# First four levels of the triangular inverse on packed 32x32 diagonal blocks, with block transposes by VectorE

## What is computed

```python
    decay = jnp.exp(jnp.where(tril, gc[..., :, None] - gc[..., None, :], -jnp.inf))
    kb = kc * bc[..., None]
    a_mat = jnp.where(strict, jnp.einsum("bhncd,bhnsd->bhncs", kb, kc) * decay, 0.0)
    eye = jnp.eye(c, dtype=jnp.float32)
    t_inv = lax.linalg.triangular_solve(eye + a_mat, jnp.broadcast_to(eye, a_mat.shape), left_side=True, lower=True)
    u = jnp.einsum("bhncs,bhnse->bhnce", t_inv, vc * bc[..., None])
    w = jnp.einsum("bhncs,bhnsd->bhncd", t_inv, kb * jnp.exp(gc)[..., None])
```

## Time and profile before

| | us |
|---|---|
| median of 3 runs (lowest, highest) | 1440.19 (1439.32, 1441.13) |
| the profiled execution's own time | 1440.25 |
| its span in the profile | 1438.5 |
| PE busy | 1350.0 (94%) |
| PEld busy | 777.8 (54%) |
| VectorE busy | 463.6 (32%) |
| ScalarE busy | 295.1 (21%) |
| GpSimd busy | 24.2 (2%) |

### The profile page before, as it was taken

One profiled execution on the slowest core, in us unless ns is written; L12 is line 12 of the kernel. 1 busy time (PEld: TensorE's weight loads), 2 busy tenths in 40 slices (PEclk: granted clock), 3 DMA queues, 4 the chain that ended last, 5 costly groups with the idle time before them and its releaser, 6 DMA issues.

```text
span 1438.5 us, 19892 instructions
## 1 busy us (share of the span) xinstructions
PE 1350.0 (94%) x7689; PEld 777.8 (54%) x7689; DVE 463.6 (32%) x1023; ACT 295.1 (21%) x629; POOL 24.2 (2%) x56
## 2 busy tenths in 40 slices
PE   8999898999999999999989899898988979999997
PEld 7887777788886444444424434254342534534355
DVE  3666877764233411211202202022020211202134
ACT  4645453444212100000001000010000100101024
POOL 3000000000000000000000000000000000000000
PEclk9999999999999999999999999999999999999998
DMA  7424243563687999999999999999999999999951
GB/s 216 137 89 127 85 136 103 165 212 99 231 288 270 402 415 421 420 420 421 421 420 420 422 421 421 421 421 422 420 421 422 421 421 415 421 422 421 420 200 31
DMA packets 123126, 463.13 MB, mean 322 GB/s; under 512 B 11142, under 2 KB 70047, under 8 KB 75311
## 3 DMA queue, kind: packets, MB, share of 16 engines
q1 hardware_dynamic: 106837, 452.99, 78.9%
q10 hardware_dynamic: 16193, 8.84, 2.1%
HBM read 455.78 MB, written 6.68 MB: 321 GB/s over the span
## 4 chain that ended last, share of the span: by engine, by line
PE 64%; DMA 16%; SPq 11%; DVE 3%; ACT 3%; issue 2%; ACTq 0%; POOL 0%; DVEq 0%; POOLq 0%
PE bank L1205 14%; DMA ring<-in_w_gate_up 13%; PE bank L1252 12%; PE bank L1012 11%; SPq L616 10%; PE bank L1144 5%; PE bank L1273 4%; PE bank L1059 3%; PE bank L834 2%; PE bank L1093 2%; PE bank L1327 2%; DMA late<-in_w_gate_up 2%; DMA dedicated<-in_w_gate_up 2%; PE bank L1191 1%; PE bank L1230 1%
## 5 line engine op out<-in xcount | busy, mean ns | idle before, releaser
L1205 PE MATMUL bank<-ring,lent 128*64 128x512 f32 (+1 forms) x1832 | 379.0, 595 | 43.5 <-DMA ring<-in_w_gate_up 43.4
L1205 PEld LDWEIGHTS bank<-ring,lent 128*64 128x64 f32 (+1 forms) x1832 | 122.0, 131 | 275.0 <-issue 274.5
L1012 PE MATMUL bank<-lent,ring 128*128 128x264 f32 x896 | 224.8, 391 | 5.1 <-ACT lent L1600 1.6
L1252 PE MATMUL bank<-ring,lent 128*64 128x512 f32 (+1 forms) x928 | 184.3, 595 | 0.0
L1012 PEld LDWEIGHTS bank<-lent,ring 128*128 128x128 f32 x896 | 160.8, 190 | 38.4 <-issue 10.2
L2159 DVE TENSOR_SCALAR big<-bank 128x512 f32<-128x512 f32 x32 | 20.6, 686 | 408.9 <-PE bank L1205 408.9
L1688 ACT ACTIVATE big<-big 128x512 f32<-128x512 f32 x32 | 19.5, 629 | 468.4 <-DVE big L2159 468.4
L1252 PEld LDWEIGHTS bank<-ring,lent 128*64 128x64 f32 (+1 forms) x928 | 56.4, 129 | 106.8 <-issue 101.3
L1144 PEld LDWEIGHTS bank<-st,big 88*128 88x128 f32 x768 | 87.0, 192 | 13.6 <-issue 12.2
L1144 PE MATMUL bank<-st,big 88*128 88x128 f32 x768 | 90.3, 277 | 0.6 <-ACT pair_space L1685 0.5
L2177 DVE TENSOR_TENSOR xT<-xT,bank 128x264 f32<-128x264 f32 x128 | 55.0, 430 | 98.5 <-PE bank L1273 97.1
(11 more groups left out here) (428 smaller groups left out, 1403.9 us busy)
## 6 DMA issues: line engine op xcount, KB each, us to landing
ring<-in_w_gate_up SPq DMA_DIRECT2D x205, 1024.0 KB, 22.0
ring<-in_w_down SPq DMA_DIRECT2D x100, 1024.0 KB, 23.9
ring<-in_w_in SPq DMA_DIRECT2D x28, 1024.0 KB, 5.3
dedicated<-in_w_gate_up SPq DMA_DIRECT2D x13, 1024.0 KB, 24.0
dedicated<-in_w_down SPq DMA_DIRECT2D x9, 1024.0 KB, 24.1
late<-in_w_gate_up SPq DMA_DIRECT2D x8, 1024.0 KB, 23.5
outputs<-in_w_gate_up SPq DMA_DIRECT2D x7, 1024.0 KB, 26.3
lent<-in_w_gate_up SPq DMA_DIRECT2D x7, 1024.0 KB, 23.6
```

The lines of the kernel that those rows point to most:

```text
L1012: last = mm(b[:, 0:T], w[:, k, o:o + P], aT[:, k, :], start=k == 0, stop=k == KD - 1)
L1205: last = mm(bank[t][lo:hi, :], x_slots[:, c, lo:hi], w, start=False, stop=c == KD - 1)
L1252: last = mm(bank[4 + t][lo:hi, :], hT[:, m, lo:hi], w, start=m == 0, stop=m == KD - 1)
```

## The change

In the levels 0 to 3 only the four diagonal 32x32 blocks of each matrix are computed. They are packed: the tile M now holds three packed arrays of 128 x 4 x 32, Mb, Db and DTb, in place of full M, Dm and DT. A step is sixteen products of 32x32x32 (four matrices, four row quarters), all into one PSUM bank. The transposes T1 and tr0 to tr3 and their ScalarE copies go; VectorE transposes the 32x32 blocks itself. After dm3 VectorE copies the blocks out of Db and DTb into Dm and DT, which GpSimd has filled with zeros. The masks are packed by GpSimd once at the start.

```diff
-GDN_PLAN = [..., ["scores"], ["tokens"], ["t1"],
-            ["ad0", "kpre"], ["dm0"], ["kap"], ["ad1", "tr0"], ["dm1"], ["skq"], ["ad2", "tr1", "sc0"], ["dm2", "sc1"], ["ob"],
-            ["ad3", "tr2", "sc2"], ["dm3", "sc3"], ["kv0"], ["ad4", "tr3"], ...
+GDN_PLAN = [..., ["scores"], ["tokens"], [],
+            ["ad0", "kpre"], ["dm0"], ["kap"], ["ad1"], ["dm1"], ["skq"], ["ad2", "sc0"], ["dm2", "sc1"], ["ob"],
+            ["ad3", "sc2"], ["dm3", "sc3"], ["kv0"], ["ad4"], ...
+QUARTERS = [slice(32 * r, 32 * (r + 1)) for r in range(4)]
...
+        def blocks_of(M):
+            return M[:, :, 0:32], M[:, :, 32:64], M[:, :, 64:96]
...
# TensorE
+            def block_products(name, lhs, rhs):
+                b = to_fill(pe, name)
+                for i in range(4):
+                    for r in QUARTERS:
+                        last = mm(b[r, 32 * i:32 * (i + 1)], lhs(i, r), rhs[r, i, :], start=True, stop=True)
+                fill_done(name, last)
...
-                elif step == "t1":
-                    pe.wait_ge(s["DT0_ready"], g + 1)
-                    transposes4(name("T1"), lambda i: DT[:, i, :])
...
                 elif step[:2] == "ad":
                     lv = int(step[2])
-                    wait_drained(pe, name(f"dm{lv - 1}" if lv else "T1"))
-                    wait_drained(pe, name("AT"))
-                    products4(name(step), lambda i: AT[:, i, :], lambda i: Dm[:, i, :])
+                    if lv:
+                        wait_drained(pe, name(f"dm{lv - 1}"))
+                    else:
+                        pe.wait_ge(s["DT0_ready"], g + 1)
+                        wait_drained(pe, name("AT"))
+                    block_products(name(step), lambda i, r: AT[r, i, r], Db)
                 elif step[:2] == "dm":
-                    if lv:
-                        wait_drained(pe, name(f"tr{lv - 1}"))
-                    products4(name(step), lambda i: DT[:, i, :], lambda i: M[:, i, :])
-                elif step[:2] == "tr":
-                    wait_drained(pe, name(f"dm{step[2]}"))
-                    transposes4(name(step), lambda i: Dm[:, i, :])
+                    wait_drained(pe, name(f"ad{step[2]}"))
+                    block_products(name(step), lambda i, r: DTb[r, i, :], Mb)
...
# VectorE
-                    tell(v.tensor_tensor(DT[:], dec[:], each4(neg_first[:]), ALU.mult))
                     tell(v.tensor_tensor(dec[:], dec[:], each4(causal[:]), ALU.mult))
                 elif step == "scores":
                     b = to_drain(dve, name("AT"))
-                    tell(v.tensor_tensor(four(DT), b[:], four(DT), ALU.mult))
-                    tell(v.tensor_tensor(DT[:], DT[:], each4(ident[:]), ALU.add), "DT0_ready")
                     out_of(v.tensor_tensor(four(AT), b[:], four(dec), ALU.mult), name("AT"))
+                    for r in QUARTERS:
+                        x = v.tensor_tensor(DTb[r], AT[r, :, r], neg_first[r, r].unsqueeze(1).broadcast_to([32, 4, 32]), ALU.mult)
+                    tell(x)
+                    tell(v.tensor_tensor(DTb, DTb, each_block(eye4[:]), ALU.add))
+                    tell(v.transpose(Db, DTb), "DT0_ready")
...
-                    out_of(v.tensor_tensor(M[:], bank4(b), each4(neg_mask[:, lv, :]), ALU.mult), name(step))
-                elif step in ("dm0", "dm1", "dm2", "dm3"):
+                    out_of(v.tensor_tensor(Mb, blocks4(b), each_block(neg_blocks[:, lv, :]), ALU.mult), name(step))
+                elif step in ("dm0", "dm1", "dm2"):
                     b = to_drain(dve, name(step))
-                    out_of(v.tensor_tensor(four(Dm), four(Dm), b[:], ALU.add), name(step))
+                    out_of(v.tensor_tensor(Db, Db, blocks4(b), ALU.add), name(step))
+                    tell(v.transpose(DTb, Db))
+                elif step == "dm3":
+                    b = to_drain(dve, name(step))
+                    tell(v.tensor_tensor(Db, Db, blocks4(b), ALU.add))
+                    tell(v.transpose(DTb, Db))
+                    for r in QUARTERS[0:2]:
+                        v.tensor_copy(Dm[r, :, r], Db[r])
+                    for r in QUARTERS:
+                        x = v.tensor_copy(DT[r, :, r], DTb[r])
+                    out_of(x, name(step))
...
# GpSimd, step "nrm", between kbg and qg
+                    if g >= 2:
+                        wait_drained(pool, f"o.{g - 2}")
+                    tell(g_.memset(DT[:], 0.0))
+                    tell(g_.memset(Dm[0:32, :, 32:64], 0.0))
```

## The result

| | before | after |
|---|---|---|
| median of 4 runs, us | 1439.76 (1439.24 to 1441.13) | 1427.14 (1425.09 to 1427.84) |
| profiled execution / its span, us | 1440.25 / 1438.5 | 1425.09 / 1423.0 |
| start of the last unbroken group of 16 projection records | 361.63 | 343.19 |
| start of the last scatter | 1389.58 | 1370.80 |

The ratio is 0.9909, with a 95% interval of 0.9893 to 0.9924: 12.6 us faster by the medians, 15.2 by the profiled executions. The forecast of 1425.4 us and its range hold the time. Its steps hold it less well: TensorE gained more than was forecast, and two things took part of it back: falls of the clock, which the prediction had as a rival at 0.02, and a second pause behind the program's branch, which it did not have.

What follows compares the result with a forecast made beforehand. TensorE was taken to set the pace of the input projections, VectorE close behind, with the whole gain passed on. 8.6 + 6.4 + 1.1 - 0.6 - 0.7 = 14.8 us off 1440.25 gave 1425.4 us, range 1417 to 1434.

Steps and rivals of the forecast that it cites:

- Full pass-through: From the projections into the expert stage: the whole gain arrives at the end, every expert mark earlier by the same amount.
- Rival (b): At the expert weight stream: already the limit before the experts, so the gain does not arrive; 1439 us, chance 0.05.
- Transposes, 8.6 us: TensorE in the delta-rule pairs: 20 groups of four transposes at 0.43 us go, all of it counts, 8.6 us gained.
- Products, 6.4 us: TensorE's 32 small-block steps: 0.70 us each instead of 0.90, 6.4 us gained, ends 2.6 and 10.9.
- (c): TensorE's small products run one behind the other: 1.15 us a step, 8.0 us lost; 1439 us, chance 0.04.
- (d): Row quarters exclude each other in one PSUM bank: 1.35 us a step, 14.4 us more; 1445 us, chance 0.03.
- T1's wait, 1.1 us: Third pair: TensorE's 1.72 us wait at T1 goes, 0.6 stays ahead of ad0, 1.1 us gained.
- dm1's waits, 0.6 us worse: Second and third pair: TensorE's waits for VectorE, 2.52 and 1.37 us, grow by 0.2 to 0.4 each; 0.6 lost.
- dm3's drain and the convolution, 0.7: VectorE's drain after dm3 takes 2.4 us, narrowly covered; with the fourth pair's convolution mean, 0.7 us subtracted.
- VectorE's new instructions: Per pair, 24 short instructions of 7.0 to 8.4 us replace 7.6 us; VectorE's total stays about the same.
- Rival (a): VectorE takes over: 2.5 us a pair more in the second to fourth pairs, 7.5 us lost; 1433 us, chance 0.13.
- rival (e): Clock falls to 1.2 GHz in the stretches of small products, adding 26 us; 1451 us, chance 0.02.

Runs made afterwards that it cites:

- both paddings: Two versions of the kernel after, with four or 64 eight-column products in the branch that never runs; 1421.8 and 1427.1 us.
- e1: The kernel after with four eight-column products written into the branch that never runs; 1421.8 us, 0.9871 of before.
- e6: The kernel after with six extra 128x128 products per pair ahead of dm4, before its wait for ad4's drain; 1426.0 us, 0.9898 of before.
- e7: The kernel after with four products in the never-run branch and dm3's six copies on ScalarE ahead of ad4's drain; 1422.9 us, 0.9885 of before.
- e12: The kernel after with four products in the never-run branch, convolution taps respread, six copies on ScalarE behind ad4's drain, waits unfilled; 1418.4 us, 0.9851 of before.
- e8: The kernel after with code position put right and TensorE's waits ahead of dm1 and dm4 filled with 128x128 products; 1420.2 us, 0.9873 of before.

## Why the prediction came out right, point by point

- **Full pass-through: right.** 18.4 us of lead at the projections' end, 18.8 at the last scatter. Rival (b) is out.
- **Transposes, 8.6 us: right.** The groups are gone, and each took its 0.43 us with it. But that is the price of the old, full-size form: given back in packed form they cost 4.8 us of TensorE, and 3.3 at the end.
- **Products, 6.4 us: mis-sized.** I took 13 ns a record and 0.70 us a step from level 4, whose records use two quarters at a time, though the same paragraph had 0.56 as the good end. Measured: 8 ns, 0.59 us, 32 x 0.31 = 9.9 us. Four quarters overlap in one bank: 8 ns against the 22 of neighbours in one quarter. Rivals (c) and (d) are out, where a step's records would have taken 0.86 us and more; they took 0.26. The rule of the Trainium skill, "TensorEngine Tiling (Array Packing)", Instruction Overhead, of some 60 cycles a matmul (by estimate 25 ns, so 0.8 us for a step's records) doesn't agree with that either, nor does its section Restrictions and Gotchas, by which row tiles can't use one bank at once.
- **T1's wait, 1.1 us: too little.** All 1.7 went: ad0 starts at 222.39 with no wait.
- **ScalarE's copies, put at nothing: too little.** ad0 waited for T1's copy too, 0.49 us in pair 2 (row below), which the prediction's list of waits leaves out with a further 0.16 ahead of ad1. Both went.
- **dm1's waits, 0.6 us worse: right in sign, too small, and one in another place.** 2.52 and 1.37 ahead of dm1 became 3.31 and 1.46, and 0.41 came up ahead of dm2 in pair 3, 1.3 us more.
- **dm3's drain and the convolution, 0.7: right in kind, half the size.** The block from L1907 to the last copy takes 2.0 us, not 2.4; what was late was not ad4 but ScalarE's drain of it (0.78, ahead of dm4), and the convolution's mean in pair 4 waited 0.74 (row below), 1.5 in all.
- **VectorE's new instructions:** the transpose takes 0.312 us, as taken, the drains 0.29 instead of 0.35 and the copies 0.22 instead of 0.3. Its total fell by 6.9 us where I had it level. Rival (a) did not come.
- **The clock, rival (e), at 0.02: it came, in small.** I looked for it in stretches of small products at full length, and it came as falls of 3 us or more in pair 2: 1.7 us in the profile of after. The argument against it rested on rows 1, whose slices are too long to show such a fall.
- **The range and the rivals' times: mis-added.** The products' ends and up to 3 us for VectorE give 1421 to 1432, not 1418 to 1431, and rival (c)'s terms give 1439.9, not 1439. Neither decides anything here.
- **The second pause at the branch: nowhere in the prediction.** 3.3 us at the end with its clock, 5 by the medians. The diff showed that TensorE's code grows; the trace of before showed the first pause.

The two waits named above, in the kernel before (pair 2) and in after (pair 4):

```profile
154.45 1.16 PE L834 MATMUL bank<-ring 128*128 128x128 f32 x8 [0.49 <-ACT ring L1520]
```

```profile
302.72 2.05 PE L1051 MATMUL bank<-lent,ones 128*128 128x264 f32 x8 [0.74 <-DVE lent L1996]
```

VectorE's groups in after, to rows 10 (count, busy us, mean ns):

```profile
L1900 DVE TENSOR_TENSOR ring<-bank,pair_space 128x128 f32<-128x128 f32 x16 | 4.7, 291 | 9.5 <-PE bank L848 9.0 <-DVE lent L1996 0.2
...
L1904 DVE STREAM_TRANSPOSE ring<-ring 128x128 f32<-128x128 f32 x12 | 3.7, 312 | 0.4
...
L1912 DVE COPY ring<-ring 32x128 f32<-32x128 f32 x16 | 3.5, 219 | 0.2
```

So at the projections' end the forecast was 14.8 us and 18.4 came, 20.1 without the clock's fall. As measured, the terms give 8.6 + 9.9 + 1.7 + 0.65 for the other two waits, less 1.3, 1.5 and 1.7 for the clock: 16.4. Another 0.5 us is the first projection record, at 13.30 instead of 13.84, which the change doesn't explain. The last 1.5 us are pieces that no wait row shows: before, a full step behind a wait took 1.00 us to the next group (165.97 to 166.96) where 0.90 is usual, and ad0 in the first pair started 0.16 late (81.99).

The code position then took 3.3 back in the profiled execution. That 1425.09 came where 1425.4 was forecast, and a median of 1427.14, is luck: two misses of opposite sign, too little trust in the overlap, and no term for what new code does to the place of old code.

## What to carry to other kernels

Count what a small tile costs in the order in which it is issued: neighbours in different row quarters overlap (8 ns a record), neighbours in one do so less or not at all (22 ns), and a group of another shape is cheap beside its like (0.30 us) and dearer alone (0.59). When code ahead of a run-time branch grows or shrinks, look at the pauses marked "issue" behind the branch before you believe a difference of 3 to 5 us, and move the code by a few instructions to see. Before you compare two profiles by a time on their axis, check that both start level: here the first projection record alone moves by 1.1 us. When an edit relieves an engine, follow the queue one engine further than the wait that it removes: whoever waits for ScalarE may be waiting for VectorE.

## What the runs showed of the hardware that I had not expected

- Records of 32x32 in four row quarters of one PSUM bank start 8 ns apart; with neighbours in one quarter 22 ns, and 32 ns where all write the same 32 columns.
- Behind a taken branch TensorE pauses once or twice, 2.1 to 2.6 us each, and 16 instructions more ahead of the target decide which. A target a few instructions ahead of the end of a 16 KB block is the reading that fits both paddings.
- The granted clock fell to 0.50 for 3 to 10 us in the middle of a stage with TensorE at work most of the time, in a kernel whose waits there are at most 0.8 us longer than before; its page shows nothing of it in slices of 36 us.
- The last scatter's 16 records (14 behind a second pause) took 5.49 to 6.22 us in before, after and e1 to e6, at a clock of 0.50 for part of them, and 3.80 at full clock in e7 to e12. Why is open.
- The clock also falls in the expert stage, amid products of 512 columns, 0.7 to 1.2 us behind waits of 2.1 to 2.2 us for a DMA (e7, e8), and stays up behind others as long.
